# First third of the adaLN matrix loaded by groups of 256 channels, and the first three feature blocks projected channel group by channel group

## The reference, cut to what matters

```python
cond = jax.nn.silu(c)                                   # (1, 1024)
mod = (cond @ ada_w[l] + ada_b[l])[:, None, :]          # ada_w: (1024, 6144)
sh1, sc1, gt1, sh2, sc2, gt2 = jnp.split(mod, 6, axis=-1)
h = rmsnorm(x, norm1_g[l]) * (1.0 + sc1) + sh1          # x: (1, 512, 1024)
proj = h @ w_in[l]                                      # w_in: (1024, 4736)
q, k, v, feat, gl = jnp.split(proj, IN_OFFSETS, axis=-1)
...
x = x + (gt1 * mixed).astype(x.dtype)
h = rmsnorm(x, norm2_g[l]) * (1.0 + sc2) + sh2
moe = expert_choice_moe(h, router_w[l], exp_w_gate[l], exp_w_up[l], exp_w_down[l])
```

## Time and profile before

| | |
|---|---|
| median of 3 runs | 1577.87 us (1575.9 to 1578.36) |
| profiled execution: device time | 1578.11 us |
| profiled execution: span | 1576.3 us |
| mean granted clock of PE | 0.963 |
| PE busy | 1410.7 us, 89% of the span |
| DVE busy | 462.6 us, 29% |
| ACT busy | 206.5 us, 13% |
| DMA queue of SP | 484.59 MB, 75.7% of 16 engines' span |

### The profile page before, as it was taken

One profiled execution on the slowest core, in us unless ns is written; L12 is line 12 of the kernel. 1 busy time (PEld: TensorE's weight loads), 2 busy tenths in 40 slices (PEclk: granted clock), 3 DMA queues, 4 the chain that ended last, 5 costly groups with the idle time before them and its releaser, 6 DMA issues.

```text
span 1576.3 us, 21762 instructions
## 1 busy us (share of the span) xinstructions
PE 1410.7 (89%) x9331; PEld 673.3 (43%) x9331; DVE 462.6 (29%) x801; ACT 206.5 (13%) x402; POOL 39.1 (2%) x45
## 2 busy tenths in 40 slices
PE   5997999999798996999989889889889889889887
PEld 1442454555666643443343343343343343343332
DVE  2799634862135624110200200200200200201102
ACT  2024001221322111110010000010010010010002
POOL 2003030000000000000000000000000000000000
PEclk9998999999899997899999999999999999999999
DMA  9952233253302365699999999999999999999995
GB/s 344 372 178 68 80 74 114 71 133 100 143 3 83 150 266 217 272 429 428 427 429 428 429 429 428 429 429 429 428 429 429 428 429 428 429 429 428 429 427 229
DMA packets 91268, 485.54 MB, mean 308 GB/s; under 512 B 36075, under 2 KB 53565, under 8 KB 62405
## 3 DMA queue, kind: packets, MB, share of 16 engines
q1 hardware_dynamic: 91149, 484.59, 75.7%
q10 hardware_dynamic: 56, 0.01, 0.0%
HBM read 470.93 MB, written 10.50 MB: 305 GB/s over the span
## 4 chain that ended last, share of the span: by engine, by line
PE 59%; DMA 29%; DVE 7%; issue 2%; ACT 1%; SPq 1%; DVEq 0%; PEldq 0%
PE psum L1156 16%; DMA arena<-in_exp_w_up_dram 14%; DMA arena<-in_exp_w_gate_dram 12%; PE psum L1171 8%; PE psum L672 6%; PE psum L584 5%; PE psum L1137 4%; DMA arena<-in_ada_w_dram 4%; PE psum L1072 3%; PE psum L993 2%; PE psum L1254 2%; PE psum L757 1%; PE psum L803 1%; DVE arena L1543 1%; SPq L280 1%
## 5 line engine op out<-in xcount | busy, mean ns | idle before, releaser
L1156 PE MATMUL psum<-arena 128*64 128x512 f32 x2048 | 472.7, 618 | 81.2 <-DMA arena<-in_exp_w_up_dram 62.2
L1156 PEld LDWEIGHTS psum<-arena 128*64 128x64 f32 x2048 | 165.0, 142 | 382.0 <-issue 381.6
L1171 PE MATMUL psum<-arena 128*64 128x512 f32 x992 | 216.2, 593 | 8.6 <-issue 6.8
L584 PE MATMUL psum<-arena 128*128 128x512 f32 x336 | 150.4, 609 | 1.4 <-DVE arena L1569 1.4
L1171 PEld LDWEIGHTS psum<-arena 128*64 128x64 f32 x992 | 83.4, 137 | 135.8 <-issue 135.6
L672 PE MATMUL psum<-arena 128*128 128x512 f32 x256 | 123.9, 606 | 0.0
L584 PEld LDWEIGHTS psum<-arena 128*128 128x128 f32 x336 | 65.0, 195 | 85.6 <-issue 82.8
L1957 DVE TENSOR_TENSOR arena<-arena,psum 128x512 f32<-128x512 f32 x32 | 19.8, 682 | 266.8 <-PE psum L1156 266.8
L1971 DVE TENSOR_TENSOR arena<-psum,arena 128x1024 f32<-128x1024 f32 x7 | 8.6, 1224 | 252.8 <-PE psum L1171 252.8
L1949 DVE TENSOR_TENSOR arena<-arena,psum 128x512 f32<-128x512 f32 x32 | 19.8, 681 | 169.2 <-ACT arena L1481 169.2
L1137 PEld LDWEIGHTS psum<-arena 128*128 128x128 f32 x512 | 63.7, 204 | 8.9 <-issue 6.5
(11 more groups left out here) (280 smaller groups left out, 1120.5 us busy)
## 6 DMA issues: line engine op xcount, KB each, us to landing
arena<-in_exp_w_gate_dram SPq DMA_DIRECT2D x64, 2048.0 KB, 25.0
arena<-in_exp_w_up_dram SPq DMA_DIRECT2D x64, 2048.0 KB, 26.7
arena<-in_exp_w_down_dram SPq DMA_DIRECT2D x62, 2048.0 KB, 27.0
arena<-in_ada_w_dram SPq DMA_DIRECT2D x24, 1024.0 KB, 10.1
arena<-in_w_in_dram SPq DMA_DIRECT2D x16, 1024.0 KB, 5.8
arena<-in_x_dram SPq DMA_DIRECT2D x2, 2048.0 KB, 8.4
gate_pre<-arena SPq DMA_DIRECT2D x16, 256.0 KB, 6.1
arena<-in_w_out_dram SPq DMA_DIRECT2D x1, 4096.0 KB, 16.4
```

The lines of the kernel that those rows point to most:

```text
L584: ins = mm(bank(b % 4), by(w_ring[g % 2], KC)[:, k, j * P:(j + 1) * P], by(hT, KC)[:, k, :], start=(k == 0), stop=(k == KC - 1))
L1156: ins = mm(bank(4 * kind + n)[e * 64:(e + 1) * 64, :], by(xeT, KC)[:, k, e * 64:(e + 1) * 64], by(ring[(j + e) % RING], 2)[:, r, n * 512:( ...
L1171: ins = mm(bank(4 + n)[e * 64:(e + 1) * 64, :], by(hidT, FBLK)[:, 4 * kk + b, e * 64:(e + 1) * 64], by(ring[(j + e) % RING], 4)[:, b, n * ...
```

## The change

The first third of `ada_w` is no longer loaded by input rows but by output channels. `ada_columns(c)` loads, for channel group pair `c` (256 channels), 256 columns of the shift and 256 of the scale, for all 1024 input rows: two DMAs of 1 MB with rows of 1 KB. The four groups have 16 KB a partition each and wait for nothing. `weights(0)` and `weights(1)` stand behind group 0, and `weights(2)` moves from between pieces 11 and 12 to behind group 3, into a place of its own (`w_early`).

On PE, `mod_rows_of(c)` makes the 512 modulation numbers of a group (8 matmuls with 32 weight columns), DVE copies them to SBUF, `mod_columns_of(c)` turns them into columns (4 matmuls of a 128x128 weight with the one column `quarter_sel`), and DVE adds the bias, now a parameter column, makes `s1` and two groups of `hT`. PE then runs `first_products(c, b)`: the matmuls of channels `2c` and `2c + 1` for blocks 0, 1 and 2, which stay open in banks 0 to 2 over all four groups. `x` comes in two halves. All 8 transposed groups of `x` are copied by ACT from PSUM into `hT`, and DVE scales them in place. Pieces 10 and 11 now wait for `mod_rows_of(3)`, piece 12 and later ones for their slots as before.

```diff
@@ sync: loads
-            load(by(x_in, TT), x[0].rearrange("(t p) d -> p t d", p=P), "x_in")
+            xt = x[0].rearrange("(t p) d -> p t d", p=P)
+            load(by(x_in, TT)[:, 0:2], xt[:, 0:2], "x_in")
+            load(by(x_in, TT)[:, 2:4], xt[:, 2:4], "late_rows_in")
+
+            def ada_columns(c):
+                dst = ada_cols[c].rearrange("p (k s n) -> p k s n", k=KC, s=2)
+                for n in range(2):
+                    o = n * D + 256 * c
+                    load(dst[:, :, n, :], ada_w[0, :, o:o + 256].rearrange("(k p) n -> p k n", p=P), f"ada_in{c}")

             def ada_piece(n):
-                if n >= 4:
-                    sp.wait_ge(sem("ada_used"), n - 3)
+                sp.wait_ge(sem("ada_used"), 2 * (n // 2 - 3) if n < 12 else n - 7)
...
-            for n in range(KC):
-                ada_piece(n)
-            for q in range(4):
-                load(adab_first[quarter(q), :], ada_b[0:1, 512 * q:512 * (q + 1)].partition_broadcast(32), "first_in")
+            ada_columns(0)
             weights(0)
             weights(1)
+            for c in range(1, 4):
+                ada_columns(c)
+            weights(2)
...
             for n in range(8, 12):
                 ada_piece(n)
-            weights(2)
             for n in range(12, 16):
                 ada_piece(n)
@@ tensor
+            def mod_rows_of(c):
+
+                pe.wait_ge(sem(f"ada_in{c}"), 32)
+                for k in range(KC):
+                    ins = mm(bank(7)[quarter(k % 4), :], cond_wide[:, 32 * k:32 * k + 32],
+                             ada_cols[c][:, 512 * k:512 * (k + 1)], start=(k < 4), stop=(k >= 4))
                 ins.then_inc(sem("ada_used"), 1)
+            def mod_columns_of(c):
+
+                pe.wait_ge(sem("modT_ready"), c + 1)
+                for j in range(4):
+                    ins = mm(bank(6)[:, 4 * c + j:4 * c + j + 1], first_rows[:, j * P:(j + 1) * P], quarter_sel,
+                             start=True, stop=True)
+                ins.then_inc(sem("mod_mm"), 1)
+
+            pe.wait_ge(sem("cond_ready"), 1)
+            mod_rows_of(0)
+            pe.wait_ge(sem("xn_ready"), TT)
+            for k in range(KC):
+                if k >= 6:
+                    pe.wait_ge(sem("xT_out"), k - 1)
                 for t in range(TT):
...
+            mod_columns_of(0)
+            def first_products(c, b):
...
+                for k in (2 * c, 2 * c + 1):
+                    if b == 0:
+                        pe.wait_ge(sem("hT_ready"), k + 1)
+                    ins = mm(bank(b), by(w_ring[g], KC)[:, k, j * P:(j + 1) * P], by(hT, KC)[:, k, :],
+                             start=(k == 0), stop=(k == KC - 1))
...
             for c in range(4):
+                for b in range(2):
+                    first_products(c, b)
+                if c < 3:
+                    mod_rows_of(c + 1)
+                first_products(c, 2)
+                if c < 3:
+                    mod_columns_of(c + 1)
...
-            for b in range(7):
+            for b in range(3, 7):
                 project(b)
@@ scalar
+            for k in range(KC):
+                act.wait_ge(sem("xT"), k + 1)
+                fn(by(hT, KC)[:, k, :], bank(k if k < 6 else k - 2), ACT.Copy).then_inc(sem("xT_out"), 1)
@@ vector
-            v.tensor_tensor(first_rows, bank(0), adab_first, ALU.add).then_inc(sem("modT_ready"), 1)
...
+            for c in range(4):
+                ks = slice(2 * c, 2 * c + 2)
+                dve.wait_ge(sem("ada_used"), c + 1)
+                v.tensor_copy(first_rows, bank(7)).then_inc(sem("modT_ready"), 1)
+                dve.wait_ge(sem("mod_mm"), c + 1)
+                s(v.tensor_tensor(mod_v[:, :, ks], by(bank(6)[:, 4 * c:4 * c + 4], 2), bias_v[:, :, ks], ALU.add))
+                s(v.scalar_tensor_tensor(s1[:, ks], mod_v[:, 1, ks], 1.0, pcol[:, N1 + 2 * c:N1 + 2 * c + 2],
+                                         ALU.add, ALU.mult))
+                for k in (2 * c, 2 * c + 1):
+                    dve.wait_ge(sem("xT_out"), k + 1)
+                    h = by(hT, KC)[:, k, :]
+                    v.tensor_scalar(h, h, s1[:, k:k + 1], modT[:, k:k + 1], ALU.mult, ALU.add) \
+                        .then_inc(sem("hT_ready"), 1)
```

More of the change, by code:

```diff
@@ L54 @@
 F32 = mybir.dt.float32
-MU0, MU1, W0, A0, KKC, KAC, RKC, LG, LB, N1, CC = 0, 15, 30, 38, 46, 50, 54, 58, 62, 66, 74
-NPAR = 82
+MU0, MU1, W0, A0, KKC, KAC, RKC, LG, LB, N1, CC, AB = 0, 15, 30, 38, 46, 50, 54, 58, 62, 66, 74, 82
+NPAR = 98
 class Signal:
@@ L137, in hybrid_layer @@
         cond_wide, first_rows = at(148, KC * 32), at(176, T)
-        adab_first, adab_rest = at(178, T), at(180, 2 * T)
+        adab_rest = at(180, 2 * T)
+        ada_cols = [at(o, 16 * KB) for o in (32, 48, 16, 64)]
+        w_early = at(168, 8 * KB)
         rest_rows = at(168, 2 * T)
@@ L257, in weights_in, with w_slot, w_sem @@
         def weights_in(g):
-            return sum(64 if n in QGROUPS else 16 for n in range(g % 2, g + 1, 2))
+            return sum(64 if n in QGROUPS else 16 for n in range(g % 2, g + 1, 2) if n != 2)
+        def w_slot(g):
+            return w_early if g == 2 else w_ring[g % 2]
+        def w_sem(g):
+            return "w2_in" if g == 2 else f"w{g % 2}_in"
         param_rows = [(MU0, shift_mu[0].rearrange("d (m p) -> (d m) p", p=P)),
@@ L291, in weights @@
             def weights(g):
-                if 2 <= g < 13:
-                    sp.wait_ge(sem("proj_mm"), 1 + max(b for b in range(len(BLOCKS)) if BLOCKS[b][0] == g - 2))
+                if 2 < g < 13:
+                    before = 0 if g == 4 else g - 2
+                    sp.wait_ge(sem("proj_mm"), 1 + max(b for b in range(len(BLOCKS)) if BLOCKS[b][0] == before))
                 elif g >= 13:
                     sp.wait_ge(sem("gate_mm"), 2 * (g - 12))
-                dst, s = w_ring[g % 2], f"w{g % 2}_in"
+                dst, s = w_slot(g), w_sem(g)
                 if g in QGROUPS:
@@ L536, in _ @@
             pe.wait_ge(sem("consts_ready"), 1)
-            pe.wait_ge(sem("params_in"), 160)
-            nc.tensor.transpose(psum[:, 0:NPAR], par_rows[0:NPAR, :], ident[0:NPAR, 0:NPAR]) \
+            pe.wait_ge(sem("params_in"), 176)
+            nc.tensor.transpose(bank(6)[:, 0:NPAR], par_rows[0:NPAR, :], ident[0:NPAR, 0:NPAR]) \
                 .then_inc(sem("params_T"), 1)
-            def mod_first(k):
-                pe.wait_ge(sem(f"ada_in{k % 4}"), 16 * (k // 4 + 1))
-                for q in range(4):
-                    ins = mm(bank(0)[quarter(q), :], cond_wide[:, 32 * k:32 * k + 32],
-                             ada_ring[k % 4][:, 512 * q:512 * (q + 1)], start=(k == 0), stop=(k == KC - 1))
-                ins.then_inc(sem("ada_used"), 1)
@@ L553, in x_transposed @@
                 ins.then_inc(sem("xT"), 1)
-            pe.wait_ge(sem("cond_ready"), 1)
-            for k in range(4):
-                mod_first(k)
-            pe.wait_ge(sem("xn_ready"), TT)
-            for k in range(7):
-                x_transposed(k)
-            for k in range(4, KC):
-                mod_first(k)
-            pe.wait_ge(sem("ada_used"), KC)
-            pe.sem_inc(sem("mod_mm"), 1)
-            pe.wait_ge(sem("modT_ready"), 1)
-            for c in range(4):
-                ins = nc.tensor.transpose(bank(0)[:, c * P:(c + 1) * P], first_rows[:, c * P:(c + 1) * P], ident)
@@ L568, in _ @@
-            ins.then_inc(sem("mod_mm"), 1)
+            mod_columns_of(0)
+            def first_products(c, b):
+                g, j = BLOCKS[b]
+                if c == 0 and j == 0:
+                    pe.wait_ge(sem(w_sem(g)), 16)
+                for k in (2 * c, 2 * c + 1):
[3 more added lines that the diff above has]
+                             start=(k == 0), stop=(k == KC - 1))
+                if c == 3:
+                    ins.then_inc(sem("proj_mm"), 1)
```

54 lines of the change are left out of this document (23 added, 31 removed).

## The result

The changed kernel takes 1588.71 us (median of 4 runs, 1586.49 to 1593.87) against 1577.72 before: ratio 1.0074, 95% interval [1.0061, 1.0087], slower. The profiled execution took 1586.49 us with a span of 1584.8, the shortest of its four; its share of the loss is 8.4 us, the median's 11.0.

A forecast was written before the change was run, and what follows sets the result against it. The prediction took the end to hang on when DVE starts ada 12, delayed by PE's loop of dependent rounds from 59.60 to 65.8 us. So 1578.1 + 6.2 = 1584.3 us, range 1577 to 1590.

The forecast's parts named there:

- rival C: PE's opening: pauses bring the low clock back once, +2.0 us, with slow mod_columns_of 1586 to 1590; chance 0.06.
- Ada 12 as the one number to watch: DVE's list: its start of ada 12, 59.60 us before, moves to 65.8 and passes to the end one to one.
- the sum: Whole kernel: 1578.1 us profiled plus 6.2 from the later start of DVE's ada 12 gives 1584.3.
- The stream: Opening loads: 1 KB rows at 350 GB/s, first third 24.0 us in place of 19.8, piece 8 landing at 50.9.
- rival B: Opening: 1 KB loads run at 424 GB/s and rounds take about 6 us, 1575.3 to 1573.8; chance 0.10.
- Rival A: Opening: the loop is shorter by 4 us or more, the stream binds, +3.1 us, 1581.2; chance 0.16.
- Group 0: PE's opening: the first group lands at 16.4 us, and the first product starts at 27.1.
- The round: PE's loop over groups: products, modulation and DVE's part take 9.2 us a round, while loads come every 6.0.
- at 20.36 to 25.4 us PE rose to the full rate under just the work that now stands first: PE's opening: given as evidence against the low clock coming back.
- Blocks 0 to 2 and what waits for them: PE's projection: blocks 0 to 2 done at 59.9 us, block 6 near 88; DVE's list covers the loras behind.
- After 152 us PE has the turn and is busy without a gap: Behind DVE's list: PE has no idle to absorb a shift, so it passes to the end one to one.
- Rival D: Behind 150 us: hidden slack absorbs the loss, or the list's start does not pass on, 1578; chance 0.10.

The follow-up runs named there:

- c0: The changed kernel once more with no edit, beside the kernel before on another chip: 1591.62 us, 1.0091.
- e1: The changed kernel with weights(2) loaded behind piece 11, not ahead of piece 8: 1590.21 us, 1.0074 of the kernel before.
- e2: The changed kernel with PE making the modulation of all four groups first, then blocks 0 to 2 each whole: 1588.4 us, 1.0069 of the kernel before.
- e8: The kernel before with 14 narrow products (56 PE instructions) added where PE idles between 144 and 151 us: 1581.42 us, 1.0022.
- e10: The changed kernel with 50 narrow products (200 PE instructions) added where PE idles ahead of kk_spread: 1586.52 us, 1.0056 of the kernel before.
- e3: The kernel before with weights(2) in a slot of its own, its load no longer waiting for block 1: 1575.76 us, 0.9987.
- e5: The kernel before with 28 identity transposes (56 PE instructions) added in PE's idle opening: 1586.44 us, 1.0057.
- e6: The changed kernel with 100 identity transposes (200 PE instructions) added in PE's opening: 1587.35 us, 1.0057 of the kernel before.

## Why the prediction was right, and where it fell short

It said slower, 1584.3 with 1577 to 1590; the median is 1588.71 and the profiled execution 1586.49, inside, and c0's 1591.62 is outside. The loss was 1.8 times the forecast 6.2 us, and the number fell inside only because the upper end of the range had been set for rival C; the 2 to 5 us lost behind kk_spread had no place in it. The direction and the mechanism of the opening were right, the size was in part luck.

*The measure.* Ada 12 as the one number to watch held: +8.75 there, +8.1 at kk_spread, and the three idle times of the earlier trace rows went as foretold. In e1, where the clock stayed up, kk_spread moved by 6.4 us against the 6.2 of the sum.

*The stream.* Right. 348 GB/s for the ada columns against 350 taken. The Trainium skill, "DMA: Bandwidth & Descriptors", Specifications, has the line rate from 512 bytes on, by which they would have moved at 424 like the 8 KB rows; the trace disagrees, so rival B had no ground. Piece 8 landed at 51.7 in e2, 50.9 predicted. Rival A needed a loop 4 us shorter; e2 had the last `hT` at 48.5 us, 6.6 before the 55.1 of the prediction, and there the stream did bind.

*Group 0.* Landed at 17.2, not 16.4. First product at 27.70, not 27.1, 0.6 us late: 0.8 of later landing less 0.3 in `mod_rows_of` (3.64, 3.9 taken), and 0.1 more in the transposes. `mod_columns_of` took 0.95 of PE, 1.0 taken; the way over DVE 1.12 and 1.03, 1.1 taken.

*The round.* 9.29 us, 9.2 taken: 0.3 in three.

*The clock.* This is the term that was mis-sized. The sum priced all products at 0.433 us; rival C held one spell of low clock, +2.0, and got a chance of 0.06. The spell came in the first profile of the change: 5.37 in place of 3.70 us, +1.67. "at 20.36 to 25.4 us PE rose to the full rate under just the work that now stands first" compared the matmuls, and left out that transposes, one-column products and two pauses come behind them. Together 0.6 + 1.67 + 0.3 - 0.2 (ada 8 follows the first product of group 3 sooner, 0.3 and not 0.5) make 57.5 for ada 8 in place of 55.2, and 0.2 more up to ada 12.

*Blocks 0 to 2 and what waits for them.* Block 2 ended at 62.5 (59.9 predicted), late by about the same (2.6 us); the loras began at 90.04, "near 88" predicted, 86.0 before. Nothing waited for it, as argued.

*"After 152 us PE has the turn and is busy without a gap", one to one to the end.* This is the step that failed. It was read in a window that ended at 196 us; I did not look at the scan, where PE already had 12.9 us of idle time with the releaser issue. Twelve more products had been priced at their own duration alone. What the runs showed in its place: up to kk_spread 7.3 to 8.1, in the scan 2.5 to 3.2 more, which is 3.6 to 3.9 of issue waits less what products and DVE gave back, and in c0 another 2 us before it, which the scatter of that stretch may be. e8 makes the second term alone, with no other part of the change (+3.3 us); e10 takes it from the change (scan 111.8 as before's 111.9). The passing on by itself held: in e3 and e2, kk_spread moved by -2.3 and +4.5 us, and the end by -2.5 and +9.0, of which 4.5 are the longer scan. Rival D, that something behind 150 us absorbs, was wrong in sign in c0; in the first profile 1.5 us came back between 556 and 649 us.

*Open.* Why one packet boundary stalls for 2.2 or 3.5 us and most of the 23 not at all was not tried. What ends the five waits that do not move, 3.45 us the longest, the profile does not show; they stand 392 or 784 records apart, which speaks for a step of the scan. Nor was it tried what brings the spell of low clock in one execution and not in the next.

## What to carry to other kernels

Breaking a wait for a load into smaller waits pays only if the work between them is not itself a chain over several engines: here three rounds of product, copy, one-column product and scaling, 9.3 us each, took the place of loads that came every 6. Find the list that the end hangs on (here DVE's), and ask of each edit when that list starts, not what the busiest engine gains. And when an edit adds or removes instructions on an engine that later issues small ones at full speed, look there for idle time put down to issue, sort the waits by whether they move with the program's length (here 8.8 of 12.9 us did not), and compare with a kernel padded to a whole packet before blaming the edit.

## What the runs showed of the hardware

- Instruction packets are not free: 23 in the 112 us of the scan, with up to three large waits (the longest 2.6 to 4.1 us) that moved by 27 or 28 records of PE (with their weight loads, 54 to 56 instructions) when 55 or 56 instructions were added and stood in their places again with 255 or 256. Only these lengths were tried. 56 instructions laid into idle time cost 3.3 us (1.3 to 3.1 per thousand), 256 cost 1.0, not told from nothing.
- Work that fills a pause can lower the clock: in e5 28 transposes ahead of the first ada products were followed by a granted clock of 0.50 to 0.68 from 12 to 24 us, where without them it was 1.00, and the list of DVE began 1.6 us later. In e6 100 transposes that ran without a pause up to the first products left it at 1.00 from 12 to 24 us, and the first `mod_rows_of` took 1.92 in place of 3.64 us, but started 3 us later.
- A product with one moving column in fp32 costs 0.119 us a record (8 in 0.95 us), little less than one with 16 columns, 0.128.
- Loads with 1 KB rows stay at 348 GB/s at a DMA share of 1.10: the queues count as full while they move a fifth less than with 8 KB rows.
